# Gate and up projections as seven Strassen block products: one core of a Trainium2 chip, 256 tokens through two encoder layers

## The reference

```python
def rms_norm(x, g):
    return x * rsqrt(mean(x * x, -1) + 1e-6) * g

def swiglu_ffn(x, w_gate, w_up, w_down):            # 1024 -> 2816 -> 1024
    return (silu(x @ w_gate) * (x @ w_up)) @ w_down

def hybrid_layer(x, ...):
    x = x + 0.5 * swiglu_ffn(rms_norm(x, ffn1_norm), ffn1_w_gate, ffn1_w_up, ffn1_w_down)
    proj = rms_norm(x, mix_norm) @ w_in
    y = concatenate([hyena_mixer(...), mla_mixer(...), gla_mixer(...)])
    x = x + y @ w_out
    x = x + 0.5 * swiglu_ffn(rms_norm(x, ffn2_norm), ffn2_w_gate, ffn2_w_up, ffn2_w_down)
    return x
```

## Time and profile before

| what | value |
|---|---|
| runs of the kernel before | 1089.90, 1089.82, 1088.97 us, median 1089.82 |
| span of the profiled execution | 1087.3 us |
| own time of the profiled execution | not listed apart; the runs lie 1.7 to 2.6 us above its span |
| TensorE, VectorE, ScalarE, GpSimd busy | 97%, 54%, 45%, 10% of the span |
| bytes moved by DMA | 178.38 MB, mean 164 GB/s |

### The profile page before, as it was taken

The page is one execution under the profiler, slowest core; times in us unless marked ns, Lnnn a source line. Parts: engine busy times, 40 slices in busy tenths (PEclk is TensorE's granted clock), DMA queues, the critical chain, the costliest instruction groups (busy, mean ns, idle before and its releaser), DMA issues.

```text
span 1087.3 us, 18211 instructions
## 1 busy us (share of the span) xinstructions
PE 1053.6 (97%) x7148; PEld 949.8 (87%) x7148; DVE 587.2 (54%) x630; ACT 493.3 (45%) x656; POOL 103.5 (10%) x165
## 2 busy tenths in 40 slices
PE   6999999999989999999989999999998999999996
PEld 6999999778768999999889999998796789999995
DVE  4644454755665654445465544457456655445544
ACT  6443344447434544443364344335555354433342
POOL 2000000330341000000010000005004210000000
PEclk9999999999979999999999999999999899999999
DMA  9565455253212455545545555554252126554551
GB/s 327 197 219 186 182 190 193 80 192 140 106 56 88 158 191 193 193 169 182 191 166 197 191 193 187 181 173 148 99 181 78 39 79 232 187 183 174 190 204 48
DMA packets 26277, 178.38 MB, mean 164 GB/s; under 512 B 3152, under 2 KB 3664, under 8 KB 5360
## 3 DMA queue, kind: packets, MB, share of 16 engines
q1 hardware_dynamic: 24912, 174.73, 44.3%
q0 software_dynamic: 880, 2.74, 0.8%
q10 hardware_dynamic: 432, 0.18, 0.1%
HBM read 176.94 MB, written 1.05 MB: 164 GB/s over the span
## 4 chain that ended last, share of the span: by engine, by line
PE 63%; issue 28%; POOL 5%; ACT 1%; DVE 1%; DMA 1%; POOLq 0%; DVEq 0%; SPq 0%; ACTq 0%
PE psum L882 20%; PE psum L883 20%; PE psum L884 20%; POOL mixer_scratch L306 3%; PE psum L1103 1%; PE psum L899 1%; DMA w_raw<-in_w_dram 1%; PE psum L972 1%; ACT w_high L367 1%; POOL statistics L283 1%; POOL mixer_scratch L333 0%; POOL mixer_scratch L338 0%; POOL statistics L293 0%; ACT mixer_scratch L438 0%; PE psum L967 0%
## 5 line engine op out<-in xcount | busy, mean ns | idle before, releaser
L588 DVE TENSOR_TENSOR w_low<-w_raw,w_high 128x2048 fp32r<-128x2048 f32 x163 | 375.3, 2305 | 245.7 <-ACT w_high L367 245.7
L882 PE MATMUL psum<-xT_high,w_high 128*128 128x256 f32 x1536 | 436.1, 284 | 5.4 <-DVE xT_low L593 4.5
L883 PE MATMUL psum<-xT_low,w_high 128*128 128x256 f32 x1536 | 434.6, 283 | 0.0
L884 PE MATMUL psum<-xT_high,w_low 128*128 128x256 f32 x1536 | 434.6, 283 | 0.0
L367 ACT ACTIVATE w_high<-w_raw 128x2048 fp32r<-128x2048 f32 x163 | 311.1, 1914 | 124.9 <-PE psum L884 119.9
L882 PEld LDWEIGHTS psum<-xT_high,w_high 128*128 128x128 f32 x1536 | 294.6, 192 | 8.9 <-DVE xT_low L593 5.3
L883 PEld LDWEIGHTS psum<-xT_low,w_high 128*128 128x128 f32 x1536 | 294.6, 192 | 1.5
L884 PEld LDWEIGHTS psum<-xT_high,w_low 128*128 128x128 f32 x1536 | 294.6, 192 | 0.0
L396 ACT ACTIVATE silu_gate<-psum 128x256 f32<-128x256 f32 x88 | 33.7, 383 | 273.1 <-PE psum L884 273.1
L882 PE MATMUL psum<-w_high,hT_high 128*128 128x512 f32 (+1 forms) x360 | 139.9, 389 | 0.0
L883 PE MATMUL psum<-w_low,hT_high 128*128 128x512 f32 (+1 forms) x360 | 139.7, 388 | 0.0
(11 more groups left out here) (163 smaller groups left out, 804.9 us busy)
## 6 DMA issues: line engine op xcount, KB each, us to landing
w_raw<-in_w_dram SPq DMA_DIRECT2D x163, 1024.0 KB, 4.8
x<-in_x_dram SPq DMA_DIRECT2D x2, 512.0 KB, 4.3
mixer_scratch<-in_fil_dram POOLq DMA_DIRECT2D x2, 512.0 KB, 6.8
out_dram<-x_normed SPq DMA_DIRECT2D x4, 256.0 KB, 2.1
mixer_scratch<-in_fil_dram POOLq DMA_DIRECT2D x2, 384.0 KB, 7.4
mixer_scratch<-in_fil_dram POOLq DMA_DIRECT2D x2, 352.0 KB, 5.9
dft<-in_dft_dram SPq DMA_DIRECT2D x1, 512.0 KB, 6.8
inverse_dft<-in_dft_dram SPq DMA_DIRECT2D x1, 512.0 KB, 6.5
```

The lines of the kernel that those rows point to most:

```text
L588: e.tensor_tensor(WL[p][:], raw[p][:], WH[p][:].bitcast(F32), ALU.subtract).then_inc(s_lo.sem, 1)
L882: e.matmul(out, ah, bh, start=start, stop=False)
L883: e.matmul(out, ah, bl, start=False, stop=False)
L884: return e.matmul(out, al, bh, start=False, stop=stop)
```

## The change

Gate and up of 512 hidden columns are now one product of x (256 x 1024) with 1024 weight columns. Both are cut in two by two blocks: x by tokens (128 each) and by features (512 each), the weights by features and into gate and up (512 columns each). Instead of eight block products, seven are made (Strassen's scheme in Winograd's form), with blocks B11, B21, B22 of the weights and four sums T1 to T4 of them. A feed-forward part has one chunk of 256 columns done directly, with all eight block products of half width, and five chunks of 512 done this way.

- **Sums of weights**: GpSimd adds two 128x2048 tiles four times a chunk (`sums`), 20 times a feed-forward part. T1 is written to a tile of its own (`NS`), the others in place, so each waits until what it overwrites has been split.
- **Slots split**: a chunk has seven product operands and two down slots, nine splits into high and low; a part has 48 where it had 33. Bytes loaded are the same.
- **Products**: a 128x128 block of x is stationary (`XOH`, `XOL`) and 512 weight columns move, 12 matmuls of 512 columns a product. x is turned before it is normalised (`turn_x`, transposes of x), scaled by the norm's gain (`scaled`), combined into S1 to S4 (`combined`), and split once a part. 1/rms goes in behind, in silu's scale and in `gate`.
- **Joins**: VectorE forms the four blocks of the result from the seven products in PSUM (`join`, seven 128x512 additions a chunk, one input in PSUM and one in SBUF). ScalarE first copies one product out (`keep`).
- **Turning hidden**: the result has tokens on the partitions, so TensorE transposes it (`turn_hidden`, eight transposes a chunk) before it is split for `down`.
- **Waits and buffers**: seven buffers for weights (`home`), four of them in the mixers' scratch. SyncE issues all loads in a written order. B11 of the next chunk is loaded when T2 has been split and T4 summed.
- **Loops**: both `Fori` loops are unrolled. The norm ahead of the mixers scales x by 1/rms on VectorE and transposes it.

The core of the diff:

```diff
-CH = FF // 256
+CHUNKS = 6
+FIRST = ["B11", "B21", "T1", "T2", "T3", "B22", "D0", "T4"]
+LATER = ["B11", "B21", "T1", "T2", "D0", "T3", "B22", "D1", "T4"]
...
+# gpsimd
+            def sums(l, f, c, names):
+                for name in names:
+                    if name == "T1":
+                        for block in ("B11", "B12"):
+                            b, k = NTH[l, f, c, block]
+                            e.wait_ge(landed[b].sem, 16 * k)
+                        if c > 1:
+                            e.wait_ge(s_lo.sem, op(l, f, c - 1, "T1") + 1)
...
+                        dst, a, b = NS, source(c, "B11"), source(c, "B12")
+                    elif name == "T3":
...
+                        e.wait_ge(landed[b].sem, 16 * k)
+                        e.wait_ge(s_t.sem, summed(l, f, c, "T1"))
+                        dst, a, b = source(c, "B12"), source(c, "B12"), source(c, "B22")
+                    elif name == "T2":
+                        e.wait_ge(s_lo.sem, op(l, f, c, "B11") + 1)
+                        e.wait_ge(s_t.sem, summed(l, f, c, "T3"))
+                        dst, a, b = source(c, "B11"), source(c, "B11"), source(c, "B12")
+                    else:
+                        e.wait_ge(s_lo.sem, op(l, f, c, "B21") + 1)
+                        e.wait_ge(s_t.sem, summed(l, f, c, "T2"))
+                        dst, a, b = source(c, "B21"), source(c, "B21"), source(c, "B11")
+                    e.tensor_tensor(dst[:], a[:], b[:], ALU.add).then_inc(s_t.sem, 1)
...
+# sync, chunk c
+                    split(op(l, f, c, "T2"))
+                    e.wait_ge(s_t.sem, summed(l, f, c, "T4"))
+                    load(l, f, c + 1, "B11")
...
+                    split(op(l, f, c, "B22"))
+                    load(l, f, c + 1, "B22")
...
+# scalar, the high part of operand n
+                if n >= RING:
+                    e.wait_ge(s_used.sem, n + 1 - RING)
+                e.activation(WH[pos(n)][:], src[:], ACT.Copy).then_inc(s_hi.sem, 1)
...
+# vector, chunk c
+                    if c > 1:
+                        join(l, f, c - 1, "C21")
+                    ffn_lo(l, f, c, "T1")
+                    if c > 1:
+                        gate(l, f, c - 1, 1)
+                    join(l, f, c, "C11")
+                    ffn_lo(l, f, c, "T2")
+                    ht_low(l, f, c - 1, 1)
+                    if c > 1:
+                        ffn_lo(l, f, c, "D0")
+                    join(l, f, c, "U2")
+                    ffn_lo(l, f, c, "T3")
+                    ffn_lo(l, f, c, "B22")
...
+                    ffn_lo(l, f, c, "D1" if c > 1 else "D0")
+                    for name in ("U3", "U4", "C22", "C12"):
+                        join(l, f, c, name)
+                    gate(l, f, c, 0)
+                    ffn_lo(l, f, c, "T4")
+                    if c + 1 < CHUNKS:
+                        ffn_lo(l, f, c + 1, "B11")
+                        ffn_lo(l, f, c + 1, "B21")
+                        ht_low(l, f, c, 0)
...
+# tensor
+            def product(l, f, c, name, bank):
+                n, o = op(l, f, c, name), OPERAND[name]
+                e.wait_ge(s_lo.sem, n + 1)
...
+                for kk in range(4):
+                    r = passes(PS[:, bank, :], XOH[o][:, kk, :], XOL[o][:, kk, :], WH[pos(n)][:, kk, :], WL[pos(n)][:, kk, :],
+                               kk == 0, kk == 3)
+                r.then_inc(s_used.sem, 1)
...
+                    product(l, f, c, "B11", x_)
...
+                    product(l, f, c, "B21", y_)
+                    turn_hidden(l, f, c - 1, 1)
...
+                    product(l, f, c, "T1", z_)
+                    e.wait_ge(s_cp.sem, kept(l, f, c))
+                    product(l, f, c, "T2", x_)
+                    if c > 1:
+                        down(l, f, c, "D0", False)
+                    e.wait_ge(s_cb.sem, joined(l, f, c, "C11"))
+                    product(l, f, c, "T3", y_)
+                    e.wait_ge(s_cb.sem, joined(l, f, c, "U2"))
...
+                    product(l, f, c, "B22", x_)
+                    down(l, f, c, "D1" if c > 1 else "D0", c == 1)
...
+                    turn_hidden(l, f, c, 0)
+                    e.wait_ge(s_cb.sem, joined(l, f, c, "U3"))
+                    product(l, f, c, "T4", y_)
```

More of the change, by code:

```diff
@@ new lines, in landings, with add @@
+def landings():
+    count, nth = [0] * 7, {}
+    def add(key, b):
+        count[b] += 1
+        nth[key] = (b, count[b])
+    for l in range(DEPTH):
+        for f in range(2):
+            if f:
+                for i in range(MIX_OPS):
+                    add((l, "mix", i), i % RING)
+            for name in ("a", "b"):
+                add((l, f, 0, name), home(0, name))
+            for c in range(1, CHUNKS + 1):
+                for name in ("B11", "B12", "B21", "B22") if c < CHUNKS else ():
+                    add((l, f, c, name), home(c, name))
+                for name in ("D0", "D1") if c > 1 else ("D0",):
+                    add((l, f, c, name), home(c, name))
+    return nth
@@ L71 @@
 NORMS = 3
-TURNS = 4
-LINKS = {"dve": 24, "pool": 49, "act": 2, "pool_start": 4}
+TURNS = 2
+XT_BANKS = [(6, 7), (0, 1)]
+HT_BANK = 7
+A11, A12, A21, A22, S1, S3, S2, S4 = range(8)
+OPERAND = {"B11": A11, "B21": A12, "T1": S1, "T2": S2, "B22": S4, "T3": S3, "T4": A22}
 class Mark:
@@ new lines, in split, with enter_mixed @@
+            def split(n):
+                e.wait_ge(s_lo.sem, n + 1)
+            def enter_mixed(l):
+                split(l * OPS + S_WO + 1)
+                load(l, 1, 0, "a")
+                e.wait_ge(a_s.sem, a_s.at(l, 2))
+                load(l, 1, 1, "B11")
+                e.wait_ge(a_o.sem, a_o.at(l, 2))
+                load(l, 1, 1, "B12")
+                split(l * OPS + S_WO + 2)
+                load(l, 1, 0, "b")
+                e.wait_ge(g_o.sem, g_o.at(l))
+                load(l, 1, 1, "B21")
+                split(l * OPS + S_WO + 3)
+                load(l, 1, 1, "B22")
@@ new lines, in _ @@
+            e.dma_start(x[:, 0, :], x_d[0:P, :]).then_inc(s_in0.sem, 16)
+            load(0, 0, 0, "a")
+            e.dma_start(x[:, 1, :], x_d[P:2 * P, :]).then_inc(s_in1.sem, 16)
+            load(0, 0, 0, "b")
+            for name in ("B11", "B12", "B22", "B21"):
+                load(0, 0, 1, name)
+            for l in range(DEPTH):
+                ffn(l, 0)
+                for i in range(RING, MIX_OPS):
+                    split(l * OPS + MIX + i - RING)
+                    mix_load(l, i)
+                enter_mixed(l)
+                ffn(l, 1)
@@ L320, in _ @@
+            for l in range(DEPTH):
+                if l == 0:
+                    x_rstd(0, 0)
+                    sums(l, 0, 1, ("T1", "T3"))
+                sums(l, 0, 1, ("T2", "T4"))
+                for c in range(2, CHUNKS):
+                    sums(l, 0, c, ("T1", "T3", "T2", "T4"))
                 x_rstd(l, 1)
@@ new lines, in down @@
+            def down(l, f, c, name, first):
+                n, h0 = op(l, f, c, name), 2 if name == "D1" else 0
+                e.wait_ge(s_lo.sem, n + 1)
+                e.wait_ge(s_hl.sem, turned(l, f, c - 1, 1))
+                for t in range(T):
+                    for h in range(2):
+                        for m in range(2):
+                            r = passes(PS[:, t * 2 + m, :], *hidden_tile(h0 + h, t), WH[pos(n)][:, h * 2 + m, :], WL[pos(n)][:, h * 2 + m, :],
+                                       first and h == 0, False)
+                r.then_inc(s_used.sem, 1)
@@ L1064, in project @@
                 return r
[L1066 to L1067 removed]
+            e.wait_ge(s_cst.sem, 16)
+            for t in range(T):
+                turn_x(0, 0, t, 0)
+                turn_x(0, 0, t, 1)
+            for l in range(DEPTH):
+                ffn(l, 0, None)
                 e.wait_ge(s_in.sem, 16 * N_IN)
```

901 lines of the change are left out of this document (604 added, 297 removed).

## The result

The kernel after the change takes 1391.01 us (median of four runs, 1385.42 to 1395.12) against 1089.39 us before: 1.277 times as long, with an interval of 1.2737 to 1.2799. The forecast was 1278 us with a range of 1190 to 1355. The direction came out as forecast, and so did the mechanism of the chunks, the turns of VectorE and GpSimd; the time lies 36 us above the range.

A forecast was written before the change was run, and what follows sets the result against it. TensorE, 97% busy, bounded the kernel before; after it, blocked turns of VectorE and GpSimd would set the pace. Stages of 240 us against 193 add 188 in four: 1087.3 + 188 = 1275, median 2.5 higher, predicted 1278; range 1190 to 1355.

The forecast's parts named there:

- Exclusion: VectorE instructions with two SBUF inputs and GpSimd instructions reading SBUF take whole turns: 39.5 us a chunk.
- waiting mostly for low parts: Sign of a right forecast: TensorE, under 80% busy, would wait mostly for VectorE's low parts of weights.
- stages near 240 us: Sign of a right forecast: each feed-forward stage near 240 us, against 193 before.
- The sums' price: GpSimd's four weight sums a chunk: 4.6 us each, 18.5 us a chunk, taken in turns with VectorE's work.
- The rival without it: Sums cost VectorE nothing: a chunk is TensorE's 31 us, the kernel 1026 us; chance 0.08.
- The order of one chunk: Hand-worked schedule of a steady chunk: 44 us, 39.5 of turns and 4.5 in which neither engine wants them.
- TensorE's part in the steady chunk: TensorE's work for a chunk of 512 hidden columns: 31 us, 3 less than before.
- turns of a stage 211; 4.5 unused in each of five chunks, 23; the last down products behind the last split, some 8: Sum for a feed-forward stage; less about 2 of the norm's latency, it gives 240 us against 193.
- Net: 16 us less a stage: TensorE's work in a feed-forward stage: fewer gate and up matmuls, less added transposes, saves 16 us.
- late loads: Other way to be wrong: loads landing later than the assumed 4.8 us, seen as ScalarE waiting for DMA.
- The clock: TensorE's clock halving behind each chunk's gap: up to 4 us a chunk, 80 in all, upper bound 1358 us.
- The mixers: Norm ahead of the mixers swaps a matmul for a scaling: nothing, bounded by 1 us each way a layer.

The follow-up runs named there:

- e3_write_only: Kernel after the change, each sum's instruction replaced by GpSimd writing a constant over the same 128x2048 tile: 1132.49 us, 1.0405 times before.
- e2_half_sums: Kernel after the change, T1 summed whole, T2 to T4 over only the first 1024 of 2048 elements of a row: 1267.07 us, 1.1611 times before.
- e1_no_sums: Kernel after the change, each sum replaced by an addition of 8 columns, products, splits and loads kept: 1137.57 us, 1.0434 times before.
- e5_late_first_sums: Kernel after the change, sums of chunk 1 wait until x's operands are split and stand behind the statistics: 1398.25 us.
- the better order: Kernel without sums, split of B21 moved up at a stage's start, join of C21 and last gate at its end: 1126.64 us, 1.0353 times before.
- e0_ports: Separate bench, not the kernel: VectorE, GpSimd and ScalarE instructions alone and together; twelve 128x2048 subtractions with six additions took 52.92 us.
- e8_sums_by_transfer: Kernel after the change, all sums made by DMA transfers that add to their destination, issued by GpSimd: 1408.47 us, 1.2934 times before.
- e12_shared_sums: Kernel after the change, reordered, T1 and T3 summed on VectorE, T2 and T4 by adding transfers: 1252.24 us, 1.1499 times before.

## Why the forecast was right and where it fell short

*Exclusion* was right: whole instructions in turn, both ways round, and not for VectorE's operations with one input in PSUM. The forecast took no side on GpSimd's writes; they do not take part. The bench shows it alone, and e3_write_only and e2_half_sums show it in the kernel. The forecast's two heaps of low parts are there (165 of 222 at 2.3, 49 at 3.7 to 6.7), TensorE is at 78%, and the joins stand at 0.68. Of its signs "waiting mostly for low parts" came half true (95.6 us for them, 138.1 for the gate, as in its own order of a chunk), and "stages near 240 us" did not come.

*The sums' price* was right in size. The rival without it was put at 1026, the forecast at 1278: 252 us. Measured: 1391.0 - 1137.6 = 253.4.

*The order of one chunk* was right: 44 us worked out, 44.6 to 45.0 measured in the second stages, with a gate held to 4.98 and TensorE idle 6.9 on average in front of the transposes (138.1 / 20), at most 7.9, where 8.4 was forecast. In the first stage of each layer two of the four steps, which hold the filter's argument too, take 46.5 to 46.6.

*TensorE's part in the steady chunk* was right: 31 us forecast, 31.4 measured without sums, against 2 x 16.98 before.

*The failed step is the sum of a stage, "turns of a stage 211; 4.5 unused in each of five chunks, 23; the last down products behind the last split, some 8", and ahead of it "Net: 16 us less a stage" for TensorE.* Both count work and take the chunk's order for the stage's; a stage's start and end, where engines wait for one another, have no term of their own but the 8. With four chunk steps of 44 and an end of 8, the 240 us leave 240 - 176 - 8 = 56 for the start. The second stage measured 72.4 for the start, 179.7 for the four steps, 13.4 for the end: 16 + 4 + 5 = 25 more; the first stage 27 + 5 + 4 = 36. Over the four stages the starts took 71 us more than that, the steps 14 and the ends 17: 102 of the 109 us by which the profiled span lies above its forecast of 1275. Two things are in the start. Without sums the forecast's stage of 193 - 16 = 177 left 177 - 4 x 31 - 8 = 45 for it, and e1_no_sums measured 56.2, with TensorE idle 9.6 of them. By VectorE's timeline x is updated, turned, scaled, combined and split by small operations before the products can use it, and the splits of B11 and B21 stand in that queue; that this queue is the cause is argued, and moving B21 up in it took only 0 to 4 us off. The first chunk's sums add 72.4 - 56.2 = 16, where the forecast had 56 - 45 = 11 for them; in the first stage the profile shows three of them each holding an operation of 0.69 for 4.6 to 5.0. e5_late_first_sums shows that moving them does not take the 16 away.

The same error stands in the forecast of the kernel without sums: 1026 against 1137.6 is 111.6 us, and 1278 against 1391.0 is 113. By size the miss is in what the forecast took for plain TensorE work, not in the sums. Without sums its stage of 177 is passed by 110 us in the four: 46 in the starts, 24 in the last chunks, 18 in the four steps with the filter's argument, which the forecast put at nothing, 19 in the ends, 3 in the rest.

*The end*: the last D0 and D1 are loaded one behind the other into one tile, each when the slot before it there has been split; ScalarE waits 4.4 and 3.5 us for them even in the better order. The forecast named late loads as a way to be wrong, but gave it no price.

*The clock* was named as the upper bound and was real (mean 0.903 against 0.987), but keeping it up in the chunks' gaps gave back only 18 us, and for the first products of a start, tried in the kernel without sums, nothing measurable. How much the rest of the half-clock time costs is open: the second wait of a start and the stages' ends (0.79 to 0.81) were not tried.

*The mixers* took 4 to 5 us more each, forecast at nothing. Part of it is the exclusion again: the next stage's first sum is made at a mixer's end and holds an operation that stands ahead of the mixer's last products. VectorE and GpSimd in the kernel after, and below them the same operation in e3_write_only, where both mixers take 146.4:

```profile
418.81 4.30 DVE L1281 TENSOR_TENSOR x_normed<-hidden,mixer_scratch 128x512 f32<-128x512 f32 x1
418.01 4.54 POOL L548 TENSOR_TENSOR mixer_scratch<-mixer_scratch 128x2048 f32<-128x2048 f32 x1
...
352.82 0.69 DVE L1281 TENSOR_TENSOR x_normed<-hidden,mixer_scratch 128x512 f32<-128x512 f32 x1
```

That is 3.6 us of the 5 between the two. The clock is another part that comes and goes: without sums one mixer takes 146.5 us at a granted clock of 1.00 and the other 153.4 at 0.93, in one and the same run. Why it falls in one of them stays open.

## What to carry to other kernels

Before work is moved to GpSimd, add the time of its instructions that read SBUF to that of VectorE's instructions with two SBUF inputs: in these runs they took turns as if on one engine, and a sum cost 4.6 us there against 2.3 on VectorE itself. On VectorE such work may be cheaper even when VectorE leads the chain. And a stage's time is its steady step times the count plus a start and an end that have chains of their own; work these out by hand like the steady step, above all where a change makes the steps fewer and longer.

## What was not expected of the hardware

- A VectorE instruction of 128x128 that meets an addition (e0_ports, five of eight at 4.47 to 4.54 us, three at 0.29) waits for the whole of it: the price goes by the number of such instructions that meet a sum, not by their size.
- GpSimd's writing of a constant over 128x2048, 1.8 us each, has no effect on VectorE's two-input operations (e0_ports: eight subtractions in 18.58 us beside it).
- An adding transfer of 1 MB between SBUF tiles takes 7.0 to 8.7 us from issue to landing (e8_sums_by_transfer, e12_shared_sums), beside 4.8 for a load of 1 MB in the kernel after, and leaves low parts at 2.3 us.
- An addition of 128x2048 alone on GpSimd takes 4.55 us (e0_ports, four in 18.21); the forecast's 4.6 was worked out from shorter ones.
